# Moving the query projections, the value product and the spread of the row sums to other places among the attention units of one stage

## The reference, cut to what matters

```python
def queries(cq, rotate):
    q = (_rms(cq) * q_norm) @ w_uq
    q = _rms(q.reshape(*q.shape[:2], MLA_HEADS, MLA_QK)) * q_gain
    return _rope_tail(q, cos, sin) if rotate else q

def keys_values(ckv, k_rope, rotate):
    ukv = ((_rms(ckv) * kv_norm) @ w_ukv).reshape(*ckv.shape[:2], MLA_HEADS, MLA_NOPE + MLA_V)
    k_nope, v = ukv[..., :MLA_NOPE], ukv[..., MLA_NOPE:]
    k_rope = jnp.broadcast_to(k_rope[:, :, None, :], (*k_nope.shape[:3], MLA_ROPE))
    k = _rms(jnp.concatenate([k_nope, k_rope], axis=-1)) * k_gain
    return (_rope_tail(k, cos, sin) if rotate else k), v
...
s = jnp.einsum('bqhd,bkhd->bhqk', qi, k).astype(jnp.float32) * scale
p = jax.nn.softmax(s, axis=-1).astype(v.dtype)
return jnp.einsum('bhqk,bkhd->bqhd', p, v)
```

## Time and profile before

| what | value |
|---|---|
| median of three runs | 3755.49 us |
| the profiled execution's own time | 3755.24 us |
| its span | 3753.4 us |
| TensorE matmuls busy | 3617.0 us, 96% |
| VectorE, ScalarE, GpSimd busy | 1746.9, 1507.3, 1278.8 us |
| the stage, first unit's turn to the last value product | 1126.17 to 1406.65 us |

### The profile page before, as it was taken

The page is one execution under the profiler, slowest core; times in us unless marked ns, Lnnn a source line. Parts: engine busy times, 40 slices in busy tenths (PEclk is TensorE's granted clock), DMA queues, the critical chain, the costliest instruction groups (busy, mean ns, idle before and its releaser), DMA issues.

```text
span 3753.4 us, 53305 instructions
## 1 busy us (share of the span) xinstructions
PE 3617.0 (96%) x19978; PEld 2911.5 (78%) x19978; DVE 1746.9 (47%) x2548; ACT 1507.3 (40%) x2525; POOL 1278.8 (34%) x540
## 2 busy tenths in 40 slices
PE   7999999999989999999999999899989999999998
PEld 5875788888867777888777788688867777877886
DVE  4766642333357765343555543411165555252114
ACT  4343432222356663232655542322245555233222
POOL 2530332232321113444333334344433323434443
PEclk9999999999999999999999999999999999999999
DMA  5358211111210002222212122222222111222222
GB/s 207 118 219 301 85 63 67 62 62 62 84 56 23 29 18 100 96 96 96 88 68 68 63 74 96 74 100 95 95 73 74 63 68 68 94 81 90 95 97 88
DMA packets 84708, 333.82 MB, mean 89 GB/s; under 512 B 9520, under 2 KB 9648, under 8 KB 78000
## 3 DMA queue, kind: packets, MB, share of 16 engines
q1 hardware_dynamic: 83808, 329.22, 25.0%
q10 hardware_dynamic: 720, 2.10, 0.2%
HBM read 329.18 MB, written 2.10 MB: 88 GB/s over the span
## 4 chain that ended last, share of the span: by engine, by line
PE 79%; issue 11%; DVE 6%; ACT 2%; POOL 2%; POOLq 0%; DVEq 0%; ACTq 0%
PE pB L276 16%; PE pB L277 16%; PE pB L278 16%; PE pB L2308 14%; POOL w_lo L2873 2%; PE pO L276 1%; PE pO L278 1%; PE pO L277 1%; PE pT L278 1%; PE pT L277 1%; PE pT L276 1%; PE pT L2366 1%; DVE arena L903 1%; PE pO L2393 1%; PE pS L2338 1%
## 5 line engine op out<-in xcount | busy, mean ns | idle before, releaser
L2873 POOL TENSOR_TENSOR w_lo<-w_raw,w_hi 128x1024 fp32r<-128x1024 f32 x520 | 1262.4, 2429 | 2351.5 <-ACT w_hi L322 2351.0
L276 PE MATMUL pB<-h_hi,w_hi 128*128 128x512 f32 x2084 | 824.3, 396 | 37.9 <-DVE h_lo L2801 15.2
L277 PE MATMUL pB<-h_lo,w_hi 128*128 128x512 f32 x2084 | 818.2, 393 | 0.0
L278 PE MATMUL pB<-h_hi,w_lo 128*128 128x512 f32 x2084 | 817.1, 392 | 0.0
L322 ACT ACTIVATE w_hi<-w_raw 128x1024 fp32r<-128x1024 f32 x520 | 547.8, 1054 | 480.5 <-PE pB L278 314.9
L276 PEld LDWEIGHTS pB<-h_hi,w_hi 128*128 128x128 f32 x2084 | 396.2, 190 | 131.3 <-issue 39.1
L278 PEld LDWEIGHTS pB<-h_hi,w_lo 128*128 128x128 f32 x2084 | 396.0, 190 | 83.6
L277 PEld LDWEIGHTS pB<-h_lo,w_hi 128*128 128x128 f32 x2084 | 396.5, 190 | 80.7 <-issue 0.7
L276 PE MATMUL pB<-b_hi,w_hi 128*128 128x512 f32 (+1 forms) x1084 | 401.0, 370 | 7.9 <-POOL w_lo L2873 6.4
L277 PE MATMUL pB<-b_lo,w_hi 128*128 128x512 f32 (+1 forms) x1084 | 396.0, 365 | 0.0
L278 PE MATMUL pB<-b_hi,w_lo 128*128 128x512 f32 (+1 forms) x1084 | 395.6, 365 | 0.0
(11 more groups left out here) (546 smaller groups left out, 5190.1 us busy)
## 6 DMA issues: line engine op xcount, KB each, us to landing
w_raw<-stream SPq DMA_DIRECT2D x520, 512.0 KB, 3.2
under<-ada SPq DMA_DIRECT2D x42, 1024.0 KB, 4.8
arena<-ada SPq DMA_DIRECT2D x6, 1024.0 KB, 17.7
x<-xT SPq DMA_DIRECT2D x1, 2048.0 KB, 8.6
out<-x SPq DMA_DIRECT2D x8, 256.0 KB, 2.1
xc<-cT SPq DMA_DIRECT2D x1, 1024.0 KB, 26.4
arena<-bmask ACTq DMA_DIRECT2D x1, 1024.0 KB, 4.9
arena<-brope ACTq DMA_DIRECT2D x2, 256.0 KB, 5.2
```

Source lines behind the costliest of these rows:

```text
L276: pe.matmul(dst, lh, rh, start=(begin and k == 0), stop=False)
L277: pe.matmul(dst, lh, rl, start=False, stop=False)
L278: last = pe.matmul(dst, ll, rh, start=False, stop=(end and k == len(pairs) - 1))
L2873: pool.tensor_tensor(w_lo[:, s, :], w_raw[:, s, :], w_hi[:, s, :].bitcast(F32), ALU.subtract).then_inc(lo_ready, 1)
```

## The change: another order of the same instructions

No instruction is added or removed, and none is changed in size. The order moves in three lists (TensorE, ScalarE, VectorE), and with it the order in TURNS_A, which decides which bank a turn gets and for whom it waits.

- The query product of the first head of the pair after next, ("Q", 2p+4), stood in slot 5 of pair p. It now stands at the head of pair p+1, ahead of its slot 0 (`turn_ahead`).
- ("AV", p-1) and ("R", p-1) stood at the end of pair p-1, R first. They now stand at the head of pair p, behind that query product, AV first. The last pair's two stay at the end, also swapped.
- ("Q", 2p+3) moves from slot 3 to slot 2; ("SK"), ("SC") from slot 2 to 3; ("SQ") stays in slot 4; the value turns of the even pairs go to slots 1, 4 and 5. The release of the keys' chunk goes from slot 6 to 5.
- On VectorE the two `dve_query_turn` go to the head of the pair and to slot 2, `dve_key_scale` of the first head from slot 3 to 4 and its `dve_key_low` from 4 to 5; `dve_key_scale` of the second head goes from slot 7 to 6; `dve_pair_scale` goes from ahead of slot 0 to behind its copy.
- On ScalarE all turns of a slot but the last go ahead of the slot's exponential.

```diff
--- before.py
+++ after.py
@@ -1623,17 +1623,23 @@
             if q == PAIRS_A:
                 return [[] for _ in range(8)]
             values = [("V", 3 * g + i) for i in range(3)] if p and p % 2 == 0 else []
-            ahead = [("Q", 2 * q + 2)] if q + 1 < PAIRS_A else []
-            return [[("K", q)], [("C", q)] + values[0:1], values[1:2] + [("SK", q), ("SC", q)], [("Q", 2 * q + 1)], [("SQ", q)],
-                    ahead, values[2:3], []]
+            return [[("K", q)], [("C", q)] + values[0:1], [("Q", 2 * q + 1)], [("SK", q), ("SC", q)], values[1:2] + [("SQ", q)],
+                    values[2:3], [], []]
+
+        def turn_ahead(p):
+
+            return [("Q", 2 * p + 2)] if 0 < p < PAIRS_A - 1 else []
 
         FIRST_TURNS = [("Q", 0), ("Q", 1), ("SR", 1), ("SR", 0), ("K", 0), ("C", 0), ("V", 0), ("V", 1), ("V", 2), ("SK", 0), ("SC", 0),
                        ("SQ", 0), ("Q", 2)]
         TURNS_A = list(FIRST_TURNS)
         for _p in range(PAIRS_A):
+            TURNS_A += turn_ahead(_p)
+            if _p:
+                TURNS_A += [("AV", _p - 1), ("R", _p - 1)]
             for _row in turns_beside(_p):
                 TURNS_A += _row
-            TURNS_A += [("R", _p), ("AV", _p)]
+        TURNS_A += [("AV", PAIRS_A - 1), ("R", PAIRS_A - 1)]
 
         def g_query(n):
             return G_HEADS + 3 * (n // 4) + n % 4 // 2
@@ -1796,6 +1802,11 @@
             pe_unit_scores(pe, 0)
             pe_unit_scores(pe, 1)
             for p in range(PAIRS_A):
+                for turn in turn_ahead(p):
+                    pe_turn(pe, turn)
+                if p:
+                    pe_turn(pe, ("AV", p - 1))
+                    pe_turn(pe, ("R", p - 1))
                 for s, beside in enumerate(turns_beside(p)):
                     u = 8 * p + s
                     if u + 2 < UNITS:
@@ -1803,14 +1814,14 @@
                     pe_unit_turn(pe, u)
                     for turn in beside:
                         pe_turn(pe, turn)
-                    if p % 2 == 0 and s == 6:
+                    if p % 2 == 0 and s == 5:
                         pe.wait_ge(k_proj, 2 * p + 4)
                         pe.wait_ge(va_proj, 3 * (p // 2) + 3)
                         pe_chunk_used(pe, g_keys(p))
                     if p + 1 == PAIRS_A and s + 1 < KD:
                         pe_out_part(pe, 0, s)
-                pe_turn(pe, ("R", p))
-                pe_turn(pe, ("AV", p))
+            pe_turn(pe, ("AV", PAIRS_A - 1))
+            pe_turn(pe, ("R", PAIRS_A - 1))
             for kt in range(KD - 1):
                 pe_out_part(pe, 1, kt)
             pe.wait_ge(a_e, UNITS)
@@ -1925,30 +1936,37 @@
             act_key_high(act, 1)
             act_hi_part(act, G_HEADS + 3)
             for p in range(PAIRS_A):
-                n, g = 2 * p + 2, G_HEADS + 3 * (p // 2)
+                for turn in turn_ahead(p):
+                    act_turn(act, turn)
+                if p:
+                    act_turn(act, ("R", p - 1))
                 for s, beside in enumerate(turns_beside(p)):
                     u = 8 * p + s
+                    n = 2 * p + 2
                     act_unit_copy(act, u)
-                    if s == 4 and p + 1 < PAIRS_A:
+                    if s == 5 and p + 1 < PAIRS_A:
                         act_key_high(act, n)
+                    for turn in beside[:-1]:
+                        act_turn(act, turn)
                     if u + 2 < UNITS:
                         act_unit_exp(act, u + 2)
-                    for turn in beside:
+                    for turn in beside[-1:]:
                         act_turn(act, turn)
                     if s == 1 and p:
                         act_pair_high(act, p - 1)
+                    g = G_HEADS + 3 * (p // 2)
                     if p + 1 < PAIRS_A:
-                        if s == 1:
+                        if s == 2:
                             act_query_high(act, n)
                         if s == 6:
                             act_query_high(act, n + 1)
+                        if s == 7:
+                            act_key_high(act, n + 1)
                         if p % 2 and s == 4:
                             act_hi_part(act, g + 6)
                         if p % 2 == 0 and s in (4, 6):
                             act_hi_part(act, g + (4 if s == 4 else 5))
-                act_turn(act, ("R", p))
-                if p + 1 < PAIRS_A:
-                    act_key_high(act, n + 1)
+            act_turn(act, ("R", PAIRS_A - 1))
             act_pair_high(act, PAIRS_A - 1)
 
         def dve_unit_max(dve, u):
@@ -2067,41 +2085,42 @@
             dve_unit_max(dve, 0)
             dve_unit_max(dve, 1)
             dve_key_low(dve, 1)
-            dve_query_rope(dve, 2)
             for p in range(PAIRS_A):
-                n = 2 * p + 2
-                if p:
+                if 0 < p < PAIRS_A - 1:
+                    dve_query_turn(dve, 2 * p + 2)
+                if p + 1 == PAIRS_A:
                     dve_pair_scale(dve, p - 1)
-                if p + 1 == PAIRS_A:
                     dve.wait_ge(av_scaled, PAIRS_A - 1)
                     dve.sem_inc(evac[2], 1)
                 for s in range(8):
                     u = 8 * p + s
+                    n = 2 * p + 2
                     if u + 2 < UNITS:
                         dve_unit_max(dve, u + 2)
                     dve_unit_copy(dve, u)
+                    if s == 0 and 0 < p < PAIRS_A - 1:
+                        dve_pair_scale(dve, p - 1)
                     if s == 1 and p:
                         dve_pair_low(dve, p - 1)
                     if s == 6:
                         dve_pair_rows(dve, p)
                     if p + 1 < PAIRS_A:
+                        if s == 0:
+                            dve_query_rope(dve, n)
                         if s == 2:
+                            dve_query_turn(dve, n + 1)
+                        if s == 3:
+                            dve_query_rope(dve, n + 1)
                             dve_query_low(dve, n)
-                        if s == 3:
+                        if s == 4:
                             dve_key_scale(dve, n)
-                        if s == 4:
+                        if s == 5:
                             dve_key_low(dve, n)
-                            dve_query_turn(dve, n + 1)
-                        if s == 5:
-                            dve_query_rope(dve, n + 1)
-                        if s == 6 and p + 2 < PAIRS_A:
-                            dve_query_turn(dve, n + 2)
+                        if s == 6:
+                            dve_key_scale(dve, n + 1)
                         if s == 7:
-                            dve_key_scale(dve, n + 1)
                             dve_query_low(dve, n + 1)
                             dve_key_low(dve, n + 1)
-                            if p + 2 < PAIRS_A:
-                                dve_query_rope(dve, n + 2)
             dve_pair_scale(dve, PAIRS_A - 1)
             dve_pair_low(dve, PAIRS_A - 1)
```

## The result

The changed kernel takes 3786.33 us (median of 4 runs, 3781.79 to 3787.68) against 3755.36: ratio 1.0083, 95% interval 1.0068 to 1.0098. The forecast was slower by 16 us, with a range up to 3781; it is slower by 31. The profiled execution took 3786.81 us, its span is 3785.0.

The account below looks back on a forecast made before the run. It took the chain from maximum to exponential to turn to copy, plus what stands between on VectorE, as the stage's limit. 3755.24 + 12.6 of waits + 3.0 of clock = 3771 us, slower by 0.4%; range 3757 to 3781.

Parts of the forecast that it names:

- K behind the scaling of AV: Slot 0, pairs 1 to 6: the key product waits for VectorE to scale AV in its bank, 1.9 us each.
- Slot 6 of the odd pairs: Next pair's first scores wait 3.6 us for the keys' low part; TensorE ready at 21.4, scores at 25.0.
- +12.6: Attention stage, all pairs and the end: sum of waits, 1.1 + 7.5 + 0.4 + 2.5 + 0.2 + 0.9 us.
- the walk itself: One odd pair followed in the new order with the earlier trace's durations: 38.1 us against 35.6, +2.5.
- The clock: TensorE at half clock behind long waits: 0 to 5 x 1.7 = 8.5 us, taken as 3.0.
- five long waits: TensorE idle 3.6 us at slot 6 in pairs 0, 1, 3, 5 and some 3 us ahead of pair 6's AV.
- Rival C: Clock drops behind all five long waits with TensorE the bound there: 12.6 + 8.5, 3776 us; chance 0.10.
- The cover of the last copy: Head of the pair: the query product covers the wait for VectorE's last copy, 1.61 us ahead of AV before.
- The end: Pair 7's first maximum pushed by scaling, +0.2 us; R behind AV delays the output projection, +0.9.

Follow-up runs that it names:

- filled kernel: Changed kernel plus unread products in TensorE's idle time ahead of K, behind slot 5's turn and ahead of the last AV wait: 3771.02 us, ratio 1.0054.
- GpSimd out of the way: Filled kernel with ScalarE's rounding of weight chunks moved to later slots, away from the keys' low part: 3768.31 us against 3771.02.
- all else undone: Changed kernel with old order within the slots and AV scaled ahead of the first maximum, new head of the pair kept: 3750.86 us, ratio 0.9999.

## Why the prediction was wrong

The direction and the places of the waits were right, and the size was half of what came: 15.6 us forecast for the stage, 33.4 measured. Two terms were too small, the clock by 11.0 us and the sum of waits by 6.7. In the sum:

- *K behind the scaling of AV*, 1.9 forecast: 1.70 to 2.01 in pairs 1 to 6. Right; undoing it alone took off 19.8 us, clock included.
- *Slot 6 of the odd pairs*, 3.6 forecast: 3.78. Right in place. The size is in part luck: the scores start 25.6 into pair 3 (25.0 forecast), 0.75 of it GpSimd's doing, and TensorE was ready 21.8 into it (21.4 forecast). Without GpSimd's part the wait would be about 3.0, an estimate from these numbers.
- *The pairs at full clock* (filled kernel): odd 38.7 (38.1 forecast), even 40.1 (38.7), pair 6 40.4 (38.7), pair 0 37.7 (37.2). The term **+12.6** is 299.8 - 280.5 = 19.3. Of the 6.7 missing, 4.9 are GpSimd: I took the low part of the keys at 0.95 from the earlier trace rows without asking what runs on GpSimd at its new place. With that taken away the odd pair is 37.9 and the scores of slot 6 start at 24.8, so the walk itself held. About 1 us in each even pair is left, and slot 6 of an even pair waits 0.91 us, in place of 1.53, with GpSimd out of the way (0.6 forecast). The value product in slot 4 makes VectorE wait 0.47 us for the scores of slot 5. This last part is read from the trace, not tested.
- *The clock*, **+3.0** forecast, 0 to 8.5 as bounds: 14.0. This is the step that failed most. I bounded it by five stretches like that of the earlier trace rows and held that what follows a wait at slot 6 is bound by VectorE. There were nine stretches, 41.0 us in all, three of them of 6.8 us; these three had begun within the wait. All five long waits were followed by half clock; three more began at K, behind waits of 1.7 to 2.0 (pairs 1, 5 and 6), and one behind the 1.53 at slot 6 of pair 4. AV of pair 6 lay in one with TensorE as its only bound. Had TensorE been the bound in all of them they would have cost 20.5, half their length, as an estimate; 14.0 of that was paid. Rival C was the right mechanism, and its price, 8.5, was itself too small by 5.5. The argument against it, that the clock held behind the 1.61 us ahead of AV, did not carry over to the new waits of the same length.
- *The cover of the last copy*: AV waits no more in pairs 0, 1, 3 and 5, as said. The gain that I put on it was right to be small: 0.55 us an odd pair with all else undone.
- *The end*: +0.89 for pair 7 and R, 1.1 forecast.

The sign of GpSimd's part was there in the trace of before. The rotation that I took at 0.99 from the earlier trace rows (1258.88) lay beside a GpSimd instruction; in the changed kernel, with none beside it, the same rotation takes 0.68. That error of 0.3 went the other way. The GpSimd instruction of before and the rotation now:

```profile
1256.93 2.39 POOL L2873 TENSOR_TENSOR w_lo<-w_raw,w_hi 128x1024 fp32r<-128x1024 f32 x1 [12.34 <-ACT w_hi L322]
```
```profile
1188.17 0.68 DVE L2000 TENSOR_TENSOR under<-under,arena 32x512 f32<-32x512 f32 x1
```

The range failed at its upper end on both counts: the clock's bound took in only waits over 3 us and one short stretch for each, and the sum of waits lacked GpSimd's part.

## What to carry to other kernels

When a product is moved, ask who reads the bank that its follower gets: a wait of 1.7 us came from one scaling put behind a maximum. Price a new idle time of TensorE at its length and again at the half clock behind it: here 19 us of waits brought 14 us of clock. And when an instruction of VectorE with two operands in SBUF is moved, look at what GpSimd does at the new place.

## What the runs showed of the hardware

- TensorE's granted clock fell behind the waits of 3.8 us in all four pairs that had one, behind waits of 1.7 to 2.0 us at K in three pairs of six, and behind one of three waits of 1.53 us; the 1.61 us ahead of AV in the kernel before left it alone in four pairs. So the length of a wait alone does not tell it; which of the shorter waits bring it down stays open. Products that nobody needs in the idle time kept it at 2.4 GHz and took 15 us off.
- VectorE's subtraction of two tiles in SBUF, beside GpSimd's, ended 0.82 us after GpSimd's did in pair 1, and took 1.57 to 1.71 us in place of 0.95; its maximum and copy out of PSUM beside the same GpSimd instruction were not slowed (0.96 and 0.55).
- Runs of one kernel spread over 3 to 11 us (the kernel before 3749 to 3758), and traces of equal code outside the stage have 81 to 96 us at half clock there.
